# Hybrid decoder block on one core: product order in the up projection, and one head's rounding order

## The chip, the cores and the metric

One of the eight cores of one Trainium2 chip. The metric is the device time of one execution in microseconds (us), the median of the runs. The profiler's recording gives one further execution, with a start and an end for each instruction on TensorE (PE for matmuls, PEld for weight loads), VectorE (DVE), ScalarE (ACT), GpSimd (POOL) and SyncE (SP, which issues DMAs).

## The reference, cut to what matters

One decoder layer over 512 tokens of width 2048, batch 1, all in float32:

```
u    = rmsnorm(x);  proj = u @ w_in               # eight heads of attention, eight of a gated recurrence, two gates
q, k = rmsnorm(q), rmsnorm(k)  per head
y_a  = stick_breaking_attention(q, k, v);  y_b = hgrn2(...)
m    = sigmoid(gate_a) * (y_a @ p_a) + sigmoid(gate_b) * (y_b @ p_b);   h = x + m @ w_o
up   = causal_depthwise_conv(rmsnorm(h) @ w_up)   # 2 x 5632 columns, width 3
out  = h + (silu(gate) * val) @ w_down
```

The change touches two places: the projection of the second head (its q and k norms), and `rmsnorm(h) @ w_up`.

## The kernel before, in words

**Split products.** Every float32 operand of a large matmul is split in two parts that the fast fp32r matmul takes exactly: ACT rounds the raw tile to its high part (`w_hi`, a copy), and DVE subtracts to get the low part (`w_lo`). A product is hi x hi, hi x lo and lo x hi, summed in a PSUM bank.

**Phase 1, heads.** Weights come in units: 128x1024 tiles (512 KB), four places in a ring. PE does 24 matmuls a unit. For each unit ACT calls `split_ahead` (L688, the copy is L686) and DVE its own (L1132, the subtraction is L1129), two units ahead (`LEAD = 2`). A head has 14 units (position `p` in `phase1_body`); a unit's load waits until the unit four before is done on PE. Beside the weights each head has its own small steps, `head_steps`, called behind the rounding of the same position. In the second head (`i == 0`, `hh == 1`) these are on ACT: position 1 squares of q (`squares_of`), 2 the inverse root for q (`inv_sqrt_start`: Ln and Exp, L754 and L756, which wait for DVE's mean, `ms`), 3 three copies for the first head and the squares of k (L760, L762, which wait for DVE's `kn`, L1331), 4 the inverse root for k, 5 the rounding of `S` (L849). On DVE, position 3: `w_lo` of the unit, take k (L1331), squares' low part, then `normed("q")`; position 4: `w_lo`, `select` and the mean of k's squares (L1209); position 5: `w_lo`, `S_lo` (L1349), `normed("k")` (L1213 to L1337). PE's q x k products (L2103) at position 6 wait for the end of `normed("k")`. ACT, DVE and PE work each through its own list in order, and meet at semaphores.

**Phase 4, feed-forward.** A table of 528 slots, each a weight tile in a ring of six. For a pair of output tiles `f` (44 of them) there are eight up slots (`kp` = 0 to 7) and then, in the middle of the run, four down slots. `f` of 7 and more are "wide": 37 of the 44. A wide up slot has seven products (a fast two-by-two scheme, `WIDE_PRODUCTS`), each a bank of its own. `wide_high` (L2268) multiplies a high weight by the high and the low activations in one matmul of 512 columns; `wide_low` (L2274) multiplies the low weight by the high activations, 256 columns into the first half of the bank. Below, "high" and "low" matmuls are these two.

- The order in a slot before: seven highs, a wait for `w_lo` (`w4_ready`), seven lows. In the last slot (`kp == 7`) three highs, three lows, a semaphore `early_done`, four highs, four lows.
- `early_done` lets ACT copy the second halves of banks 0 to 2 (`low_halves`, L1006) and DVE add the first halves (`add_halves`, L1785) while the other four banks are still written; behind the slot's end the same is done for banks 3 to 6 (L1001). Then DVE combines, scales and convolves.
- The down slots (L2359, L2360, L2363, 512 columns each) use banks 7, 0, 1, 7; ACT copies each out (L1037), and the GpSimd queue adds it to `out_t` in HBM.
- SP loads slot `n` once slot `n - 6` is done (L469). DVE at position `n`: for an even slot `n + 3` of a wide `f`, the weight sums of that slot and the next in three operations (L1743, L1746, L1748), which wait for both loads; then `lo_slot(n + 2)` (L1755). So at the position of `kp` = 1 DVE waits for the loads of `kp` = 4 and 5, and only then subtracts `w_lo` for `kp` = 3. ACT rounds `w_hi` three slots ahead (L965).

Of the kernel before, what the change touches and what calls it, by code (L numbers as in the profile page):

```python
# [27 lines left out]
P = 128  # L28
# [19 lines left out]
HEAD_UNITS = 14  # L48
HEAD_TILES = 7
HEADS_PER_BODY = 2  # L50
BODY1 = HEADS_PER_BODY * HEAD_UNITS
# [16 lines left out]
KP = KT // 2  # L68
# [57 lines left out]
EARLY = 3  # L126
# [34 lines left out]
def build_program(nc, x_t, wstream, wgates, wslots, wfirst, params, out_t):  # L161
# [7 lines left out]
    def sb(name, cols, at, dt=F32):  # L169
        return nc.alloc_sbuf_tensor_at(name, [P, cols], dt, offset=base + at)  # L170
# [76 lines left out]
    w4_hi = [sb(f"w4_hi{j}", WC, a + 4 * WC, F32R) for j, a in enumerate(ring_at)]  # L247
# [41 lines left out]
    bank = [banks[:, j * SEQ:(j + 1) * SEQ] for j in range(8)]  # L289
# [50 lines left out]
    w4_step, w4_sums, w4_hi_ready, w4_ready, slot_done = (  # L340
        sem("w4_step"), sem("w4_sums"), sem("w4_hi_ready"), sem("w4_ready"), sem("slot_done"))
    p1_ready, up_out, first_out, a_ready, dve4_step = (
        sem("p1_ready"), sem("up_out"), sem("first_out"), sem("a_ready"), sem("dve4_step"))
    early_done, low_copied, drained = sem("early_done"), sem("low_copied"), sem("drained")
# [93 lines left out]
    def part(t, j, n=1):  # L438
        return t[:, j * HALF:(j + n) * HALF]
# [18 lines left out]
    with nc.Block() as block:  # L458
# [221 lines left out]
        def _(act):  # L680
            steps = Steps(act, act_step)

            def split_hi(n, slot, arrived):
                act.wait_ge(w_in_slot[slot], arrived)
                act.wait_ge(unit_done, n + 1)
                act.activation(w_hi[slot][:, :], w_raw[slot][:, :], ACT.Copy).then_inc(w_hi_ready, 1)  # L686

            def split_ahead(start, i, body, p):  # L688

                q = p + LEAD  # L690
                before = PAIR_SLOTS if start >= START_P else 0
                if isinstance(i, int):
                    n = start + i * body + q
                    if WSLOTS + 1 < n < START4:
                        split_hi(n, n % WSLOTS, 16 * ((n - before) // WSLOTS + 1))
                else:
                    assert start % WSLOTS == 0 and body % WSLOTS == 0
                    split_hi(i * body + (start + q), q % WSLOTS,
                             i * (16 * body // WSLOTS) + 16 * ((start + q - before) // WSLOTS + 1))
# [160 lines left out]
            def phase1_body(i):  # L860
                for hh in range(HEADS_PER_BODY):
                    for p in range(HEAD_UNITS):
                        split_ahead(0, i, BODY1, hh * HEAD_UNITS + p)
                        if not i == hh == 0:
                            head_steps(i, hh - 1, HEAD_UNITS + p)
                        head_steps(i, hh, p)

            for i in range(HEADS // HEADS_PER_BODY):
                phase1_body(i)
# [1118 lines left out]
        def _(pe):  # L1988
# [262 lines left out]
            def bank_free(f, j):  # L2251

                d = GROUP * (f - 3)
                if f == WIDE:
                    if j >= GROUP:
                        pe.wait_ge(down_out, GROUP + d + j - GROUP + 1)
                    return
                pe.wait_ge(drained, 2 * (f - WIDE) - (j < EARLY))
                if j < 2:
                    pe.wait_ge(down_out, GROUP + d + j + 2)  # L2260

            def wide_high(f, kp, ring, j):

                w, x = WIDE_PRODUCTS[j]
                both = v_parts[kp][:, :].rearrange("p (a c) -> p a c", a=2)[:, :, x * HALF:(x + 1) * HALF]
                if kp == 0:
                    bank_free(f, j)
                nc.tensor.matmul(bank[j].rearrange("p (a c) -> p a c", a=2), w4_hi[ring][:, w * P:(w + 1) * P], both,  # L2268
                                 start=kp == 0, stop=False, skip_group_check=True)

            def wide_low(kp, ring, j):

                w, x = WIDE_PRODUCTS[j]
                return nc.tensor.matmul(bank[j][:, 0:HALF], w4_lo[ring][:, w * P:(w + 1) * P], part(v_hi[kp], x),  # L2274
                                        start=False, stop=kp == KP - 1, skip_group_check=True)

            def wide_products(at_, f, kp, ring):

                for j0, j1 in ((0, EARLY), (EARLY, 7)) if kp == KP - 1 else ((0, 7),):
                    for j in range(j0, j1):  # L2280
                        wide_high(f, kp, ring, j)
                    if j0 == 0:
                        pe.wait_ge(w4_ready, at_ + 1)
                    for j in range(j0, j1):
                        ins = wide_low(kp, ring, j)
                    if j1 == EARLY:
                        ins.then_inc(early_done, 1)
                return ins

            def down_free(d):  # L2290
# [15 lines left out]
            def up_slot(n):  # L2306
                _, f, kp = entry(n)
                at_, ring, loads = place(n)
                if f == 0:
                    pe.wait_ge(v_ready, kp + 1)  # L2310
                if f == 1 and kp == 0:
                    pe.wait_ge(rms_ms, 2)
                if f > 1 and kp == 0:
                    pe.wait_ge(up_out, (f - 1))
                if wide(f):
                    pe.wait_ge(w4_hi_ready, at_ + 1)
                    wide_products(at_, f, kp, ring).then_inc(slot_done, 1)
                    return
                pe.wait_ge(w4_ready, at_ + 1)
                for w, x, b, half in PRODUCTS:  # L2320
                    out = bank[4 * (f == 1) + b][:, half * HALF:(half + 1) * HALF]
                    wh, wl = (t[ring][:, w * P:(w + 1) * P] for t in (w4_hi, w4_lo))
                    xh, xl_ = (t[kp][:, x * HALF:(x + 1) * HALF] for t in (v_hi, v_lo))
                    nc.tensor.matmul(out, wh, xh, start=kp == 0 and half == 0, stop=False, skip_group_check=True)  # L2324
                    nc.tensor.matmul(out, wh, xl_, start=False, stop=False, skip_group_check=True)  # L2325
                    ins = nc.tensor.matmul(out, wl, xh, start=False, stop=kp == KP - 1, skip_group_check=True)  # L2326
                ins.then_inc(slot_done, 1)
# [146 lines left out]
```

## Time and profile before

| | |
|---|---|
| median of 3 runs | 2783.75 us (2783.39 to 2783.79) |
| profiled execution: own time, span | 2783.4 us, 2781.9 us |
| granted TensorE clock | 1.000 |
| busy: PE, DVE, ACT | 2775.1, 2109.6, 1285.3 us |
| L2268 high matmuls, 2072 | 531.0 us busy |
| L2274 low matmuls, 2072 | 300.5 us busy |

The span is the time from the first to the last instruction of the recording; what lies around it is 1.5 us. Busy time is the union of an engine's instructions. Matmuls are pipelined and overlap in the rows: a high one lasts 0.39 us in its row while the next starts some 0.23 us behind it. What a matmul takes of the time is therefore read from one start to the next.

### The profile page before, as it was taken

Reading aid. Unit: us, or ns where it says so; the run is one execution under the profiler, and the core shown is the slowest. Engines: PE = TensorE matmul, PEld = TensorE weight load, DVE = VectorE, ACT = ScalarE, POOL = GpSimd, SP = SyncE. Lnnn points to the kernel's source line nnn. Section 1 sums busy time; section 2 is a strip of 40 time slices with the busy share of each in tenths; the row PEclk is TensorE's granted clock in tenths of the full one; section 3 lists DMA queues with packets and bytes.
Section 4 is the critical chain, followed back from the end, with each engine's and each line's share of the span. In section 5 each row is a group of like instructions: output and inputs, shape, how many; then the busy total and the mean of one; then the engine's idle time right before and its main releaser. Section 6 shows DMA issues by size and latency. Waiting matters only on the chain.

```text
span 2781.9 us, 41114 instructions
## 1 busy us (share of the span) xinstructions
PE 2775.1 (100%) x14858; PEld 2403.7 (86%) x14858; DVE 2109.6 (76%) x3543; ACT 1285.3 (46%) x1738; POOL 428.2 (15%) x579
## 2 busy tenths in 40 slices
PE   9999999999999999999999999999999999999999
PEld 7888888888889999888889988888888888888887
DVE  7776777677777878444468988888888888888884
ACT  5444434443433334333345555555555555555554
POOL 2022154324400000000000110111101011110102
PEclk9999999999999999999999999999999999999999
DMA  5464586676534555444455666556556666655657
GB/s 181 144 178 96 176 189 137 176 192 125 112 118 153 168 177 176 143 143 143 137 168 145 149 141 138 139 136 144 135 138 140 138 139 135 144 136 137 140 138 163
DMA packets 187446, 410.97 MB, mean 148 GB/s; under 512 B 22288, under 2 KB 50320, under 8 KB 186128
## 3 DMA queue, kind: packets, MB, share of 16 engines
q1 hardware_dynamic: 120240, 283.90, 33.0%
q0 software_dynamic: 67040, 124.82, 23.8%
q8 instruction: 109, 1.79, 0.3%
q14 instruction: 57, 0.47, 0.0%
HBM read 347.81 MB, written 112.72 MB: 166 GB/s over the span
## 4 chain that ended last, share of the span: by engine, by line
PE 97%; DVE 2%; ACT 1%; issue 0%; DMA 0%; SPq 0%; DVEq 0%; ACTq 0%
PE bank L2268 17%; PE bank L1995 12%; PE bank L1997 12%; PE bank L1996 12%; PE bank L2274 9%; PE bank L2359 6%; PE bank L2360 6%; PE bank L2363 6%; PE bank L2221 3%; PE bank L2222 3%; PE bank L2223 3%; PE bank L2324 2%; PE bank L2326 2%; PE bank L2325 2%; PE bank L2069 1%; PE bank L2103 1%
## 5 line engine op out<-in xcount | busy, mean ns | idle before, releaser
L965 ACT ACTIVATE w_hi<-w_two 128x896 fp32r<-128x896 f32 (+1 forms) x528 | 434.3, 839 | 358.3 <-DVE w_two L1748 311.9
L2268 PE MATMUL bank<-v_parts,w_hi 128*128 128x512 f32 x2072 | 531.0, 392 | 0.0
L1755 DVE TENSOR_TENSOR w_lo<-w_two,w_hi 128x896 fp32r<-128x896 f32 (+1 forms) x528 | 495.9, 952 | 25.4 <-ACT w_hi L965 24.6
L2268 PEld LDWEIGHTS bank<-v_parts,w_hi 128*128 128x128 f32 x2072 | 370.2, 189 | 63.5
L1995 PE MATMUL bank<-u_hi,w_hi 128*128 128x512 f32 x1000 | 395.4, 395 | 0.2 <-DVE w_lo L1129 0.2
L1997 PE MATMUL bank<-u_hi,w_lo 128*128 128x512 f32 x1000 | 389.9, 390 | 0.0
L1996 PE MATMUL bank<-u_lo,w_hi 128*128 128x512 f32 x1000 | 389.3, 389 | 0.0
L1129 DVE TENSOR_TENSOR w_lo<-w_raw,w_hi 128x1024 fp32r<-128x1024 f32 x189 | 230.4, 1222 | 133.4 <-ACT w_hi L686 131.3
L668 POOL DMA_DIRECT2D out_t<-stage x168 | 142.6, 851 | 1161.9 <-ACT stage L1037 1129.5
L2274 PEld LDWEIGHTS bank<-v_parts,w_lo 128*128 128x128 f32 x2072 | 292.4, 190 | 26.3
L2274 PE MATMUL bank<-v_parts,w_lo 128*128 128x256 f32 x2072 | 300.5, 282 | 0.0
L2359 PE MATMUL bank<-s_hi,w_hi 128*128 128x512 f32 x698 | 272.1, 390 | 0.9 <-ACT stage L1037 0.9
L2360 PE MATMUL bank<-s_lo,w_hi 128*128 128x512 f32 x698 | 272.1, 390 | 0.0
L1997 PEld LDWEIGHTS bank<-u_hi,w_lo 128*128 128x128 f32 x1000 | 187.7, 188 | 40.0
L1995 PEld LDWEIGHTS bank<-u_hi,w_hi 128*128 128x128 f32 x1000 | 187.9, 188 | 38.2 <-DVE w_lo L1129 0.8
L1996 PEld LDWEIGHTS bank<-u_lo,w_hi 128*128 128x128 f32 x1000 | 187.9, 188 | 37.7 <-issue 0.2
L686 ACT ACTIVATE w_hi<-w_raw 128x1024 fp32r<-128x1024 f32 x189 | 197.1, 1048 | 16.2 <-DMA w_raw<-wstream 16.1
L2363 PE MATMUL bank<-s_hi,w_lo 128*128 128x512 f32 x698 | 189.1, 389 | 0.0
L1743 DVE TENSOR_TENSOR w_two<-w_two 128x512 f32<-128x512 f32 (+1 forms) x180 | 115.3, 641 | 65.6 <-DMA w_two<-wslots 64.5
L2359 PEld LDWEIGHTS bank<-s_hi,w_hi 128*128 128x128 f32 x698 | 131.2, 188 | 27.2 <-issue 1.3
L2363 PEld LDWEIGHTS bank<-s_hi,w_lo 128*128 128x128 f32 x698 | 131.0, 188 | 27.2
L878 ACT ACTIVATE g_hi<-g_raw 128x896 fp32r<-128x896 f32 x96 | 91.1, 951 | 137.1 <-DVE g_raw L1572 101.4
(303 smaller groups left out, 5266.5 us busy)
## 6 DMA issues: line engine op xcount, KB each, us to landing
w_two<-wslots SPq DMA_DIRECT2D x504, 256.0 KB, 2.7
w_raw<-wstream SPq DMA_DIRECT2D x189, 512.0 KB, 3.5
out_t<-stage POOLq DMA_DIRECT2D x168, 256.0 KB, 4.3
sums_scratch<-wfirst POOLq DMA_DIRECT2D x72, 448.0 KB, 5.6
g_raw<-sums_scratch SPq DMA_DIRECT2D x48, 448.0 KB, 3.3
g_raw<-wgates SPq DMA_DIRECT2D x48, 256.0 KB, 2.9
w_two<-sums_scratch SPq DMA_DIRECT2D x24, 448.0 KB, 3.3
sums_scratch<-sums_scratch POOLq DMA_DIRECT2D x72, 128.0 KB, 4.5
```

The costliest lines, as they stand in the source:

```text
L686: act.activation(w_hi[slot][:, :], w_raw[slot][:, :], ACT.Copy).then_inc(w_hi_ready, 1)
L965: act.activation(w4_hi[ring][:, 0:width], w4_raw[ring][:, 0:width], ACT.Copy).then_inc(w4_hi_ready, 1)
L1129: dve.tensor_tensor(w_lo[slot][:, :], w_raw[slot][:, :], w_hi[slot][:, :].bitcast(F32), ALU.subtract).then_inc(w_ready, 1)
L1755: dve.tensor_tensor(w4_lo[ring][:, 0:width], w4_raw[ring][:, 0:width], w4_hi[ring][:, 0:width].bitcast(F32), ALU.subtract).then_inc(w4_rea ...
L1995: nc.tensor.matmul(out, wh, hi, start=first, stop=False)
L1996: nc.tensor.matmul(out, wh, lo, start=False, stop=False)
L1997: return nc.tensor.matmul(out, wl, hi, start=False, stop=last)
L2268: nc.tensor.matmul(bank[j].rearrange("p (a c) -> p a c", a=2), w4_hi[ring][:, w * P:(w + 1) * P], both, start=kp == 0, stop=False, skip_gr ...
L2274: return nc.tensor.matmul(bank[j][:, 0:HALF], w4_lo[ring][:, w * P:(w + 1) * P], part(v_hi[kp], x), start=False, stop=kp == KP - 1, skip_g ...
L2359: nc.tensor.matmul(out, wh, s_hi[f % 8][:, :], start=first and f == fs[0], stop=False)
L2360: nc.tensor.matmul(out, wh, s_lo[f % 8][:, :], start=False, stop=False)
L2363: ins = nc.tensor.matmul(out, w4_lo[ring][:, k * P:(k + 1) * P], s_hi[f % 8][:, :], start=False, stop=last and f == fs[-1])
```

## The change

Phase 1, ACT: in the second head the roundings for positions 3 and 5 are called at positions 2 and 4, ahead of these positions' `head_steps`. Phase 4, PE: in wide up slots of odd `kp` the seven lows come first, then the seven highs; in the last slot (`kp == 7`) `early_done` is set by the third high. Even slots keep their order. The start and stop flags go along. No instruction is added or removed.

```
--- before.py
+++ after.py
@@ phase1_body, ACT
-                        split_ahead(0, i, BODY1, hh * HEAD_UNITS + p)
+                        early = i == 0 and hh == 1
+                        if not (early and p in (3, 5)):
+                            split_ahead(0, i, BODY1, hh * HEAD_UNITS + p)
+                        if early and p in (2, 4):
+                            split_ahead(0, i, BODY1, hh * HEAD_UNITS + p + 1)
                         if not i == hh == 0:
                             head_steps(i, hh - 1, HEAD_UNITS + p)
                         head_steps(i, hh, p)
@@ wide_high, wide_low: PE
-    nc.tensor.matmul(..., start=kp == 0, stop=False, ...)
+    return nc.tensor.matmul(..., start=kp == 0, stop=kp == KP - 1, ...)
...
-                                        start=False, stop=kp == KP - 1, skip_group_check=True)
+                                        start=False, stop=False, skip_group_check=True)
@@ wide_products: PE
-                for j0, j1 in ((0, EARLY), (EARLY, 7)) if kp == KP - 1 else ((0, 7),):
-                    for j in range(j0, j1):
+                if kp % 2 == 0:
+                    for j in range(7):
                         wide_high(f, kp, ring, j)
-                    if j0 == 0:
-                        pe.wait_ge(w4_ready, at_ + 1)
-                    for j in range(j0, j1):
+                    pe.wait_ge(w4_ready, at_ + 1)
+                    for j in range(7):
                         ins = wide_low(kp, ring, j)
-                    if j1 == EARLY:
-                        ins.then_inc(early_done, 1)
+                else:
+                    pe.wait_ge(w4_ready, at_ + 1)
+                    for j in range(7):
+                        wide_low(kp, ring, j)
+                    for j in range(7):
+                        ins = wide_high(f, kp, ring, j)
+                        if kp == KP - 1 and j == EARLY - 1:
+                            ins.then_inc(early_done, 1)
                 return ins
```

## Rows read from the trace of the kernel before

**Rows 1.** Page, part 1: busy us (share of the span) and instructions of PE.

```profile
PE 2775.1 (100%) x14858; PEld 2403.7 (86%) x14858; DVE 2109.6 (76%) x3543; ACT 1285.3 (46%) x1738; POOL 428.2 (15%) x579
```

**Rows 2.** Waits of PE: us in total, times, longest.

```profile
PE bank L2103 <- DVE kn L1337: 1.1, 1, 1.1
PE bank L2359 <- ACT stage L1037: 0.9, 1, 0.9
```

**Rows 3.** Timeline (start us, us, engine), PE: slots kp 0 to 3 of f = 20.

```profile
2003.34 1.75 PE L2268 MATMUL bank<-v_parts,w_hi 128*128 128x512 f32 x7
2004.92 1.00 PE L2274 MATMUL bank<-v_parts,w_lo 128*128 128x256 f32 x7
2005.75 1.78 PE L2268 MATMUL bank<-v_parts,w_hi 128*128 128x512 f32 x7
...
2010.65 1.78 PE L2268 MATMUL bank<-v_parts,w_hi 128*128 128x512 f32 x7
```

**Rows 4.** Timeline, PE: first and sixth matmul of the down slot behind f = 20.

```profile
2022.88 0.40 PE L2359 MATMUL bank<-s_hi,w_hi 128*128 128x512 f32 x1
...
2024.04 0.39 PE L2360 MATMUL bank<-s_lo,w_hi 128*128 128x512 f32 x1
```

**Rows 5.** Timeline, DVE and PE: second gate slot, which starts at 844.23, all 256 columns.

```profile
842.97 2.09 DVE L1576 TENSOR_TENSOR g_lo<-g_raw,g_hi 128x896 fp32r<-128x896 f32 x2 [4.35 <-ACT g_hi L878]
...
844.23 0.33 PE L2221 MATMUL bank<-u_hi,g_hi 128*128 128x256 f32 x1
844.40 0.28 PE L2222 MATMUL bank<-u_lo,g_hi 128*128 128x256 f32 x1
844.52 0.28 PE L2223 MATMUL bank<-u_hi,g_lo 128*128 128x256 f32 x1
```

**Rows 6.** Timeline, DVE, f = 20: first weight sum for kp 4, 5; low part for kp 3.

```profile
2007.62 0.69 DVE L1743 TENSOR_TENSOR w_two<-w_two 128x512 f32<-128x512 f32 x1 [1.67 <-DMA w_two<-wslots]
...
2009.15 1.08 DVE L1755 TENSOR_TENSOR w_lo<-w_two,w_hi 128x896 fp32r<-128x896 f32 x1
```

**Rows 7.** Timeline, DVE and PE, f = 31: the same two, and the start of slot kp 3.

```profile
2343.61 0.69 DVE L1743 TENSOR_TENSOR w_two<-w_two 128x512 f32<-128x512 f32 x1 [2.63 <-DMA w_two<-wslots]
...
2345.14 1.08 DVE L1755 TENSOR_TENSOR w_lo<-w_two,w_hi 128x896 fp32r<-128x896 f32 x1
...
2345.63 1.78 PE L2268 MATMUL bank<-v_parts,w_hi 128*128 128x512 f32 x7
```

**Rows 8.** Timeline, ACT, last f: the copy out of bank 7 that a down slot waits for.

```profile
2731.85 0.58 ACT L1037 ACTIVATE stage<-bank 128x512 f32<-128x512 f32 x1
```

**Rows 9.** Timeline, ACT, second head: root of q, rounding, squares of k, rounding.

```profile
122.11 0.63 ACT L754 ACTIVATE rs<-ms 128x512 f32<-128x512 f32 x1 [8.54 <-DVE ms L1209]
...
123.31 1.04 ACT L686 ACTIVATE w_hi<-w_raw 128x1024 fp32r<-128x1024 f32 x1
...
126.25 0.63 ACT L760 ACTIVATE sq<-kn 128x512 f32<-128x512 f32 x1 [1.08 <-DVE kn L1331]
...
136.46 1.04 ACT L686 ACTIVATE w_hi<-w_raw 128x1024 fp32r<-128x1024 f32 x1
```

**Rows 10.** Timeline, DVE, second head: two low parts that wait, and k's last step.

```profile
124.39 1.23 DVE L1129 TENSOR_TENSOR w_lo<-w_raw,w_hi 128x1024 fp32r<-128x1024 f32 x1 [2.31 <-ACT w_hi L686]
...
137.54 1.22 DVE L1129 TENSOR_TENSOR w_lo<-w_raw,w_hi 128x1024 fp32r<-128x1024 f32 x1 [2.31 <-ACT w_hi L686]
...
142.39 0.75 DVE L1337 SCALAR_TENSOR_TENSOR kn<-kn,par,tmp 128x512 f32<-128x512 f32 x1
```

**Rows 11.** Timeline, PE, second head: before k's squares, k's squares, q x k.

```profile
127.91 0.39 PE L1997 MATMUL bank<-u_hi,w_lo 128*128 128x512 f32 x1
128.33 0.50 PE L2040 MATMUL bank<-sq_hi,ones_r 128*128 128x512 f32 x1
...
143.20 2.42 PE L2103 MATMUL bank<-qn,kn 128*128 128x512 f32 x8 [1.15 <-DVE kn L1337]
```

**Rows 12.** Page, part 6: issues of one form, KB each, median us from issue to landing.

```profile
w_raw<-wstream SPq DMA_DIRECT2D x189, 512.0 KB, 3.5
```

More of the change, by code:

```diff
@@ L2267, in wide_high @@
                     bank_free(f, j)
-                nc.tensor.matmul(bank[j].rearrange("p (a c) -> p a c", a=2), w4_hi[ring][:, w * P:(w + 1) * P], both,
-                                 start=kp == 0, stop=False, skip_group_check=True)
+                return nc.tensor.matmul(bank[j].rearrange("p (a c) -> p a c", a=2), w4_hi[ring][:, w * P:(w + 1) * P],
+                                        both, start=kp == 0, stop=kp == KP - 1, skip_group_check=True)
             def wide_low(kp, ring, j):
```

## The prediction, made before the changed kernel was run

> **What bounds the kernel now.** I read the page's busy times first, then the waits of PE, then PE's timeline by starts. PE is busy 2775.1 us of a span of 2781.9 [rows 1], so nothing but PE's own list and its few stalls can move the time. The waits of PE hold two of about a microsecond: q x k in the second head waits 1.1 us for k's last step, and a down slot of the last f waits 0.9 us for a copy of ACT [rows 2]. Everything else must come from the spacing of the matmuls. A faster DVE or ACT is worth nothing unless one of these waits ends on it. The sum is made against the profiled execution's own 2783.4 us (the span and 1.5 around it), 0.35 below the median shown; I add 0.35 at the end.
>
> **Part 1, spacing of highs and lows.** From start to start, seven highs that follow 512-column matmuls (kp 0) take 2004.92 - 2003.34 = 1.58 us, and the seven lows behind them 0.83; slots kp 1 and 2, whose highs follow lows, take (2010.65 - 2005.75) / 2 = 2.45, against 2.41 for kp 0 [rows 3]. So a switch from low to high costs about 0.03 us (on finer starts 0.026, spent over the first five highs). The down slots confirm it: their first five matmuls behind the lows take 1.16 us, where five at the pace of the kp 0 highs (0.227) are 1.13 [rows 3, 4]. Lows in a long run go at 0.12 each [rows 5], seven are 0.84, so the seven right behind highs gain 0.01. A pair of switches taken away is therefore worth 0.03 - 0.01 = 0.02.
>
> Before, a wide f had eight such pairs that cost (kp 0 to 7; the extra one inside kp 7 makes that slot no longer than the others). After, highs and lows come in runs of fourteen: four pairs. Four pairs at 0.02 are 0.08 us per f, and 37 wide f give 37 x 0.08 = 3.0 us. Bounds: the 10 ns of the rows allow 0.015 to 0.025 a pair, 2.2 to 3.7 us; and nothing, if kp 0's pace had another reason (a rival below).
>
> By the Trainium skill ("TensorE: Matmul & The Clock Gate", section "Back-to-back issue gap") the isolated gap is N/2.4 + 2.5 ns, which depends on the columns alone: an estimate of 109 and 216 ns in any order, and so nothing gained by this part. The trace has 0.227 and 0.12 and a pace that depends on what went before, so I go by the rows; the rule's consequence stands among the rivals.
>
> **Part 1, the wait that moves forward.** In odd slots `w_lo` is needed at the slot's start, seven highs (1.6 us) earlier. Behind the first low stands all of PE's list. What is ready by then? For kp 0, 2, 4, 6 nothing changes. For kp 1 the low part ends 0.9 to 1.7 us ahead of the slot's start over the 37 f, for kp 7 1.7 us or more. For kp 3 DVE is held up by the loads for kp 4 and 5: it waits 1.67 us for them, sums, and ends `w_lo` for kp 3 at 2009.15 + 1.08 = 2010.23, while the slot starts at 2010.65 [rows 3, 6]: 0.42 us to spare. In f = 31 the load is later (the wait is 2.63) and `w_lo` ends at 2346.22 for a slot that starts at 2345.63: 0.59 too late [rows 7]. The spare time of the 37 kp 3 slots, from pairs of rows like these, has a median of 0.45; six are below 0.2: 0.17, 0.03, -0.12, -0.14, -0.15 and -0.59. The new order brings slot kp 3 0.02 us closer (two switches less on the way). The chain is tied to the end of the slot before kp 0 (which lets the load of kp 5 go), so a stall in one f buys nothing in the next. Slots kp 5 have 0.03 to 0.04 more than kp 3 in every f, and a stall at kp 3 gives them as much again: no second stall.
>
> How early must `w_lo` be there? The nearest row: in the second gate slot, in a run of 256-column matmuls as here, the low part ended near 842.97 + 1.08 = 844.05, 0.18 us ahead of the slot's start at 844.23, and the next matmul came 0.17 behind, where the pace is 0.12 [rows 5]: 0.05 lost. So about 0.22 is needed. The loss is 0.24 minus the spare time: 0.07 + 0.21 + 0.36 + 0.38 + 0.39 + 0.83 = 2.2 us. Bounds: nothing, if the loads land well in that run (their landings vary from run to run), and 5 us with twice as many late ones.
>
> **Part 1, `early_done`.** In kp 7 it used to come after three highs and three lows, 1.05 us into the slot; now after seven lows and three highs, 0.84 + 0.70 = 1.54. ACT's copy of the early banks starts about 0.48 later; behind it are ACT's next rounding and the copy of the late banks, which used to start 0.2 us after the slot's end and will start 0.33 later. DVE's additions move by as much, 0.35. In 36 f DVE's idle wait for the loads (1.67) [rows 6] takes this up, and kp 1 keeps 0.5 us of its 0.9. In the last f the chain runs through to the copy out at 2731.85 [rows 8], for which PE waits 0.9 us [rows 2]: that stall grows by 0.35 us. Bounds 0 to 0.5.
>
> **Part 2, second head.** The wait of 1.15 us ahead of q x k [rows 11] ends with k's last step, 142.39 + 0.75 [rows 10]. Walk it back. DVE's `w_lo` waited 2.31 us twice, at 124.39 and 137.54 [rows 10], both times for a rounding on ACT that stood behind roots (123.31 and 136.46) [rows 9]. ACT had stood idle 8.54 us before the roots of q [rows 9], and the raw tile is there: its load, issued when unit 15 ended (105.3), takes 3.5 us [rows 12]. So the first rounding, 1.04, fits into this idle time near 113.5 and delays no root. Then DVE goes on at 122.1: `w_lo` to 123.3, take k to 123.9; ACT, with its roots and the three copies until 124.2, squares k then instead of at 126.25 [rows 9]. Normed q ends near 129.4 (was 131.5). The second rounding needs unit 21's tile (issued at 120.3, there at 123.8) and goes at 126.4, again in idle time. DVE's position 4 ends at 133.1 (was 135.2), the root of k at 134.4, `S_lo` at 136.5, and normed k at 139.9 instead of 143.1. PE is ready for q x k at 141.9 at the latest, so the stall goes whole, and 2 us of cover remain. No queue is passed: the roundings issue no DMA, and the loads on SP are released by PE.
>
> The price of a stall is more than its wait: behind it the next matmuls are slow as after a switch. k's squares started 0.42 behind the last matmul [rows 11] where the pace is 0.23, 0.19 lost and some 0.13 after it; the first product with `S` lost a little over 0.2 in this way; q x k 1.3 and 0.1 after it. All three inputs come 1.7 us or more earlier. Together 1.9 us gained. Bounds: 1.1 (the wait alone) to 2.1.
>
> **Sum.** 2783.4 - 3.0 + 2.2 + 0.35 - 1.9 = 2781.05, and with 0.35 for the median 2781.4.
>
> **Rivals.**
> - *Late low weights in nearly every f* (not faster). If PE, which takes instructions in ahead of their turn, has to have `w_lo` some 0.6 us ahead, the typical spare 0.42 [rows 3, 6] falls short by 0.2 in 37 f (7 us), and the late six bring 2 more than counted. It decides from a need of 0.35 on. For it: DVE is within half a microsecond in most f. Against it: the gate slot lost 0.05 at 0.18 to spare [rows 5]. Time: 2783.75 - 3.0 - 1.9 + 0.35 + 2.2 + 6 to 7 = about 2788.
> - *The order is worth nothing*: kp 0's highs are quick for another reason than what precedes them, and the fourteen-runs go at the old pace. The down slots' slow first five [rows 4] speak against it. Time: 2781.4 + 3.0 = 2784.4. This is also what the skill's gap rule ("Back-to-back issue gap") would give.
> - *No late loads*: DMA landings in that run leave kp 3 in time everywhere. Time: 2781.4 - 2.2 = 2779.2. The typical f has time to spare [rows 6], but six outliers in 37 are not likely to vanish together.
> - *Part 2 does nothing*, because k's chain is then held by another step. Its cover of 2 us speaks against it. Time: 2783.3.
>
> **Chances.** Forecast 0.58, late nearly everywhere 0.12, order worth nothing 0.08, no late loads 0.18, part 2 idle 0.04. Range 2779.0 to 2785.0: it holds the forecast with both bounds of most terms, the second, third and fourth rival, and leaves out the first and part of the extremes. A change below 0.2% (5.6 us, 2778.2 to 2789.3) can't be told from none with this measurement; all cases lie inside, so 0.92 for the same; faster needs gains beyond every bound, 0.05; slower a first rival with a need of 0.8 us, 0.03.
>
> **What would show it.** In PE's timeline: highs of even slots starting as 1.58 us for seven, fourteen lows near 1.67, a wide f 0.08 us shorter where nothing stalls; waits of PE on `w_lo` L1755 (shifted by the new lines), few and all at kp 3; no wait for `kn`; the wait of the last f near 1.3. Wrong would be: waits on `w_lo` in most f, stalls at kp 1, or an even slot's highs still taking 1.61.

## The result and the profile after

| | before | after |
|---|---|---|
| median of 22 runs each | 2783.6 us (2783.02 to 2784.05) | 2787.5 us (2785.0 to 2788.99) |
| profiled execution: own time, span | 2783.4, 2781.9 us | 2788.83, 2787.3 us |

The ratio is 1.0014, 95% interval 1.0008 to 1.002. The change costs 3.9 us (0.14%), and the interval doesn't reach 1. The result is outside the forecast range (2779.0 to 2785.0), and close to what the first rival gave (2788). The granted clock is 1.000 in both.

The page of after, its span and the busy times of the engines, answers to [rows 1]:

```profile
span 2787.3 us, 41262 instructions
PE 2778.0 (100%) x14858; PEld 2405.9 (86%) x14858; DVE 2103.7 (75%) x3543; ACT 1278.5 (46%) x1738; POOL 428.0 (15%) x579
```

The waits of PE in after (total us, times, longest us) answer to [rows 2]:

```profile
PE bank L2278 <- DVE w_lo L1759: 2.5, 4, 1.1
PE bank L2368 <- ACT stage L1041: 1.3, 1, 1.3
```

The wait for `kn` is gone and the last f's is 1.3, both as forecast. New are four waits for `w_lo`, 2.5 us. These four can't explain a run that is about 8.5 us above the forecast without stalls (worked out below). The rest shows only in the starts. PE's timeline of f = 20 in after (start, us, line, count) answers to [rows 3]; the last row is cut by the window:

```profile
2003.58 1.75 PE L2272 MATMUL bank<-v_parts,w_hi 128*128 128x512 f32 x7
2005.16 1.84 PE L2278 MATMUL bank<-v_parts,w_lo 128*128 128x256 f32 x14
2006.84 3.36 PE L2272 MATMUL bank<-v_parts,w_hi 128*128 128x512 f32 x14
2010.04 2.12 PE L2278 MATMUL bank<-v_parts,w_lo 128*128 128x256 f32 x14
2011.99 2.23 PE L2272 MATMUL bank<-v_parts,w_hi 128*128 128x512 f32 x9
```

The lows of `kp` 0 and 1 take 2006.84 - 2005.16 = 1.68 us, as forecast. The lows of `kp` 2 and 3, same count and same columns, take 2011.99 - 2010.04 = 1.95. The 0.27 us between them is a stall at the first low of `kp` 3. The view of waits doesn't list it, since a matmul's row overlaps its successor's start by about 0.17 us and no clear idle time is left. On starts, 36 of the 37 wide f stall there: the eight up slots of an f take 19.77 us in the mean, where the one f that doesn't stall (f = 41) takes 19.49 and an f of before 19.55.

The chain that makes `w_lo` late, f = 20 of before (ACT, DVE and GpSimd; in square brackets the idle time before and what ended it). With [rows 6] it is complete:

```profile
1992.08 0.96 DVE L1785 TENSOR_TENSOR early_sum<-bank,early_sum 128x768 f32<-128x768 f32 x1 [1.82 <-ACT early_sum L1006]
2000.29 0.69 DVE L1851 TENSOR_TENSOR a_gate<-a_gate,r_tok 128x512 f32<-128x512 f32 x1
2001.01 0.82 ACT L1019 ACTIVATE y_gate<-a_gate,par 128x512 f32<-128x512 f32 x1 [1.14 <-DVE a_gate L1851]
2001.73 0.58 ACT L1037 ACTIVATE stage<-bank 128x512 f32<-128x512 f32 x1
2002.60 0.85 POOL L668 DMA_DIRECT2D out_t<-stage  x1 [2.43 <-ACT stage L1037]
```

and the same chain in after, whose last two rows answer to [rows 6]:

```profile
1992.83 0.96 DVE L1789 TENSOR_TENSOR early_sum<-bank,early_sum 128x768 f32<-128x768 f32 x1 [2.62 <-ACT early_sum L1010]
2000.89 0.69 DVE L1855 TENSOR_TENSOR a_gate<-a_gate,r_tok 128x512 f32<-128x512 f32 x1
2001.61 0.82 ACT L1023 ACTIVATE y_gate<-a_gate,par 128x512 f32<-128x512 f32 x1 [1.13 <-DVE a_gate L1855]
2002.33 0.58 ACT L1041 ACTIVATE stage<-bank 128x512 f32<-128x512 f32 x1
2003.21 0.85 POOL L668 DMA_DIRECT2D out_t<-stage  x1 [2.43 <-ACT stage L1041]
2008.32 0.69 DVE L1747 TENSOR_TENSOR w_two<-w_two 128x512 f32<-128x512 f32 x1 [1.85 <-DMA w_two<-wslots]
2009.85 1.08 DVE L1759 TENSOR_TENSOR w_lo<-w_two,w_hi 128x896 fp32r<-128x896 f32 x1
```

Against the start of the f's first up slot (2003.34 before, 2003.58 after) the early addition goes from -11.26 to -10.75, DVE's scaling (`a_gate`) from -3.05 to -2.69, ACT's third copy out of the down slots from -1.61 to -1.25, and its store to `out_t` from -0.74 to -0.37. The loads that DVE waits for are issued as before (+0.34 for the second), yet they land later: the weight sums start at +4.74 where they started at +4.28. `w_lo` for `kp` 3 ends at 2010.93; the slot would have started at 2010.04 + 7 x 0.12 = 2010.88.

So the new `early_done` reaches the loads: through DVE's scaling, ACT's convolution term, the copy that stands behind this term in ACT's list, and a store that now overlaps a load more. That is theory A. Theory B says that the order of the products itself makes `w_lo` late, by an earlier need or by what PE does to the loads, and `early_done` is a bystander.

The second head in after. DVE answers to [rows 10], PE to [rows 11].

```profile
132.61 1.22 DVE L1133 TENSOR_TENSOR w_lo<-w_raw,w_hi 128x1024 fp32r<-128x1024 f32 x1
138.71 0.75 DVE L1341 SCALAR_TENSOR_TENSOR kn<-kn,par,tmp 128x512 f32<-128x512 f32 x1
```
```profile
127.53 0.39 PE L2001 MATMUL bank<-u_hi,w_lo 128*128 128x512 f32 x1
127.75 0.39 PE L2044 MATMUL bank<-sq_hi,ones_r 128*128 128x512 f32 x1
140.94 2.32 PE L2107 MATMUL bank<-qn,kn 128*128 128x512 f32 x8
```

ACT in the second head of after answers to [rows 9]; each row holds two roundings, the position's own and the one moved ahead:

```profile
112.15 2.00 ACT L686 ACTIVATE w_hi<-w_raw 128x1024 fp32r<-128x1024 f32 x2
124.92 1.99 ACT L686 ACTIVATE w_hi<-w_raw 128x1024 fp32r<-128x1024 f32 x2
```

Normed k ends at 139.46 instead of 143.14, and DVE's two waits of 2.31 are gone. k's squares follow 0.22 behind the last matmul, where it was 0.42, and q x k starts 143.20 - 140.94 = 2.3 us earlier, with no stall. Not all of this is the change: the start of an execution varies by a microsecond (the 51st matmul of PE starts at 13.00 us in before, at 12.63 in after, and between 12.35 and 13.67 over all traces here), and these 0.4 us are still there at the 501st. From the 501st to the 701st matmul, with the second head's stalls between them, before takes 159.14 - 112.71 = 46.43 us and after 156.79 - 112.31 = 44.48: the head is worth 1.95 us.

### The profile page after: what moved, and what is told of

It reads as the page before. It is cut to its first block, busy times and chain, and to the rows that moved or that the text cites. A ratio compares the mean times of both kernels' runs of the same rounds, so it can differ in the third digit from the quotient of the medians.

```text
span 2787.3 us, 41262 instructions
## 1 busy us (share of the span) xinstructions
PE 2778.0 (100%) x14858; PEld 2405.9 (86%) x14858; DVE 2103.7 (75%) x3543; ACT 1278.5 (46%) x1738; POOL 428.0 (15%) x579
## 4 chain that ended last, share of the span: by engine, by line
PE 96%; DVE 2%; DMA 1%; ACT 1%; issue 0%; SPq 0%; DVEq 0%
PE bank L2272 16%; PE bank L1999 12%; PE bank L2001 12%; PE bank L2000 12%; PE bank L2278 9%; PE bank L2368 6%; PE bank L2369 6%; PE bank L2372 6%; PE bank L2225 3%; PE bank L2227 3%; PE bank L2226 3%; PE bank L2333 2%; PE bank L2335 2%; PE bank L2334 2%; PE bank L2073 1%; DMA w_two<-wslots 1%
## 5 line engine op out<-in xcount | busy, mean ns | idle before, releaser
L2272 PE MATMUL bank<-v_parts,w_hi 128*128 128x512 f32 x2072 | 503.7, 391 | 0.0
L2272 PEld LDWEIGHTS bank<-v_parts,w_hi 128*128 128x128 f32 x2072 | 379.5, 188 | 72.7
L2278 PEld LDWEIGHTS bank<-v_parts,w_lo 128*128 128x128 f32 x2072 | 269.8, 191 | 19.9 <-ACT w_hi L969 7.0
L2278 PE MATMUL bank<-v_parts,w_lo 128*128 128x256 f32 x2072 | 278.6, 284 | 3.2 <-DVE w_lo L1759 2.5
L2369 PEld LDWEIGHTS bank<-s_lo,w_hi 128*128 128x128 f32 x698 | 131.0, 188 | 27.0
```

What stands on the lines that cost most here:

```text
L2272: return nc.tensor.matmul(bank[j].rearrange("p (a c) -> p a c", a=2), w4_hi[ring][:, w * P:(w + 1) * P], both, start=kp == 0, stop=kp == K ...
L2369: nc.tensor.matmul(out, wh, s_lo[f % 8][:, :], start=False, stop=False)
```

## The experiments

Each kernel was timed beside the kernel before, on the same chip. Diffs are against the kernel after, unless said otherwise. Event times below are medians over the 37 wide f, against the start of the first up slot; "sums" is the start of the weight sums for `kp` 4 and 5, which is 0.09 us after the later of their two loads has landed, wherever DVE waits for it.

**The parts apart.** First the second head alone (phase 4 as before):

```
             def wide_products(at_, f, kp, ring):
-                if kp % 2 == 0: ...                    # the new order
+                for j0, j1 in ((0, EARLY), (EARLY, 7)) if kp == KP - 1 else ((0, 7),):
...
```

> The kernel before with the second head's two roundings moved ahead, the up projection as before. Two theories on the change's 10 us of lost time in the wide slots. Theory A (store meets load): early_done comes 0.5 us later, so DVE's additions and scaling end 0.36 later, so ACT's copy out behind the gate's conv term, and the store it lets go, are 0.36 later and run beside the load for kp 5, which lands 0.4 later and makes the low part for kp 3 late in nearly every f. Theory B (order itself): the lows in front need their weights earlier, or slots of the new order let loads and DVE go later, wherever early_done stands. Both theories leave the head out, so both expect here: no wait for kn, PE 2.3 us ahead by the end of the heads (from the trace of the changed kernel: 1083.56 against 1081.2 at the projections behind the gates), no change later. 2783.6 - 2.3 = 2781.3 us.

Measured: 2781.65 us (2781.03 to 2781.99) beside 2783.57, ratio 0.9993 (0.9984 to 1.0002). The profile has no wait for `kn` and 0.9 in the last f; from the 501st to the 701st matmul it takes 44.44 us. The interval reaches 1, but all eleven runs lie below all those of before beside them (2783.05 to 2784.23). Part 2 is worth the 1.9 us of the forecast, so part 1 must have cost what is missing. Then the order alone (roundings of the second head as before):

```
-                        early = i == 0 and hh == 1
...
+                        split_ahead(0, i, BODY1, hh * HEAD_UNITS + p)
```

> The kernel before with the up projection's new order, the second head as before. Both theories: the wide slots as in the changed kernel, 36 of 37 f stall at kp 3 for 0.27 us in the mean (10 us), 3.0 us gained by fewer switches, 0.35 lost in the last f, and the head's 1.1 us wait for kn is back. 2787.5 + 2.3 = 2789.8 us.

Measured: 2787.72 us (2786.42 to 2790.42), ratio 1.0015 (1.0006 to 1.0024); q x k waits 1.2 us for `kn` again. That is 4.15 above before, 2 us less than expected. The expectation put the head at 2.3 instead of 1.95. The stalls of its profiled execution were smaller (the up slots of the 37 wide f take 729.5 us, in after 731.4). Loads land differently from run to run; the interval on each of these ratios is 2.5 us wide to either side, so whether the parts really fail to add up stays open.

**`early_done` late, order untouched.** Before, with the semaphore set two highs later in the last slot, which is nearly when the change sets it:

```
# against the kernel before
                     for j in range(j0, j1):
-                        wide_high(f, kp, ring, j)
+                        ins = wide_high(f, kp, ring, j)
+                        if j0 == EARLY and j == EARLY + 1:
+                            ins.then_inc(early_done, 1)
...
-                    if j1 == EARLY:
-                        ins.then_inc(early_done, 1)
```

> The kernel before with one difference: in the last up slot early_done is set two high matmuls later (behind the fifth high, about 0.46 us later), the order of products unchanged. Theory A: DVE's additions 0.3 to 0.36 us later, the third store of an f as much later, the loads for kp 5 land 0.4 later, the low part for kp 3 ends about 0.45 us later against the slot's start (0.47 to spare falls to about 0); since the highs still come first in kp 3, PE does not stall, but for the last f's wait (0.9 to about 1.3): 2783.6 + 0.3 = 2783.9 us. Theory B: load landings and the low part for kp 3 as before, 0.47 to spare.

```profile
2002.04 0.58 ACT L1037 ACTIVATE stage<-bank 128x512 f32<-128x512 f32 x1
2002.91 0.85 POOL L668 DMA_DIRECT2D out_t<-stage  x1 [2.42 <-ACT stage L1037]
2007.73 0.69 DVE L1743 TENSOR_TENSOR w_two<-w_two 128x512 f32<-128x512 f32 x1 [1.55 <-DMA w_two<-wslots]
2003.33 1.75 PE L2268 MATMUL bank<-v_parts,w_hi 128*128 128x512 f32 x7
```

Measured: 2783.96 us (2783.3 to 2784.78), ratio 1.0002 (0.9993 to 1.0011). The old order needs `w_lo` only behind the highs, so the time can't move; the events can, and do. In f = 20 above the copy starts at -1.29 and the store at -0.42; over all f the sums go from 4.24 to 4.60, and `w_lo` would stand a median 0.10 us ahead of slot `kp` 3, where it stood 0.47. With the products in the old order, the late semaphore alone brings the loads in 0.37 us later. Theory A holds here; B has no place for this.

**The copy ahead of the convolution term.** If the delay passes through the copy's place behind ACT's term, then moving the term behind the copy must cut it:

```
-                    if q == KP + 2:
-                        conv_term(n, f, 0)
...
+                        conv_term(n, f, 0)             # one position later, behind the third copy
```

> The changed kernel with one difference on ACT: for f of 6 to 42 the gate's conv term moves from position kp + 2 behind the slots to position kp + 3, behind that position's copy out, so that the third copy out of an f no longer waits for DVE's scaling. Theory A: the third copy starts about 1.3 us earlier (near -2.5 us from the start of kp 0 instead of -1.25), its store is mostly through when the load for kp 5 is issued, the load lands in 2.7 to 3.3 us instead of 4.3, the low part for kp 3 is in time, no or few waits of PE on w_lo: 2783.6 - 2.3 - 3.0 + 0.35 = 2778.7 us. Theory B: the stalls stay, 2787.5 us.

```profile
2000.14 0.60 ACT L1041 ACTIVATE stage<-bank 128x512 f32<-128x512 f32 x1 [0.58 <-PE bank L2371]
2001.03 0.85 POOL L668 DMA_DIRECT2D out_t<-stage  x1 [1.18 <-ACT stage L1041]
2002.66 1.75 PE L2271 MATMUL bank<-v_parts,w_hi 128*128 128x512 f32 x7
2006.86 0.69 DVE L1746 TENSOR_TENSOR w_two<-w_two 128x512 f32<-128x512 f32 x1 [1.22 <-DMA w_two<-wslots]
```

Measured: 2781.17 us (2779.83 to 2783.02), ratio 0.9991 (0.9982 to 1.0). The copy now waits for PE and no longer for DVE, the store goes at -1.63 and the sums start at 3.96. The median stall is gone, but in the profiled execution four f (9, 12, 28, 31) still lose 3.9 us together. That execution took 2783.02, the slowest of the eleven; without these stalls it would be at 2779.1, near the expected 2778.7 (which put the head at 2.3 instead of 1.95), so such stalls are the likely reason for the miss. One edit on ACT, far from PE, recovers 6.3 us of the change: theory B can't say why.

**Less in the last slot.** `kp` 7 as three lows, three highs, `early_done`, four lows, four highs, so that the semaphore comes as early as before:

```
-                    for j in range(7):
-                        wide_low(kp, ring, j)
-                    for j in range(7):
-                        ins = wide_high(f, kp, ring, j)
+                    for j0, j1 in ((0, EARLY), (EARLY, 7)) if kp == KP - 1 else ((0, 7),):
+                        for j in range(j0, j1):
+                            wide_low(kp, ring, j)
+                        for j in range(j0, j1):
+                            ins = wide_high(f, kp, ring, j)
...
```

> The changed kernel with the last up slot in the order three lows, three highs, early_done, four lows, four highs, so that early_done comes 1.06 us into the slot as in the kernel before (instead of 1.54). Theory A: DVE's additions, the third store (issued 0.735 us ahead of kp 0) and the landing of the load for kp 5 (weight sums at about 4.25) go back to the times of before, and the loss at kp 3 falls from 0.27 us per f to that of the late outliers, 2 to 4 us in all; the last f's wait is 0.9 again: 2783.6 - 1.9 (head) - 2.7 (switches) + 2 to 4 = 2781 to 2783 us. Theory B (the order itself makes the weights late): stalls as in the changed kernel, 2787.5 us.

```profile
2000.13 0.85 POOL L668 DMA_DIRECT2D out_t<-stage  x1 [2.42 <-ACT stage L1041]
2000.85 1.75 PE L2272 MATMUL bank<-v_parts,w_hi 128*128 128x512 f32 x7
2004.95 0.69 DVE L1747 TENSOR_TENSOR w_two<-w_two 128x512 f32<-128x512 f32 x1 [1.48 <-DMA w_two<-wslots]
2007.31 1.84 PE L2278 MATMUL bank<-v_parts,w_lo 128*128 128x256 f32 x14
2008.98 3.36 PE L2272 MATMUL bank<-v_parts,w_hi 128*128 128x512 f32 x14
```

Measured: 2780.7 us (2779.56 to 2782.6), ratio 0.999 (0.9981 to 0.9999). Store at -0.72, sums at 4.20, the lows of `kp` 2 and 3 in 1.67 again, the last f's wait back at 0.9. Six f stall (19, 29, 31, 32, 33, 37; about 2.5 us), and the prediction counted six and 2.2 us for loads that land as in before. This is the order of the change with `early_done` where it was, and it does what the forecast said.

**The order of DVE.** In after the subtraction for `kp` 3 stands behind the sums, which wait for the loads. Put ahead of them, the loads don't matter to it:

```
+                if wide(f) and q == 1:
+                    lo_slot(n + 2)
+                    sums(n + 3)
+                else:
...
```

> The changed kernel with one difference on DVE: at the position of kp 1 in wide f the low part for kp 3 comes ahead of the weight sums of kp 4 and 5, so it no longer waits for the load for kp 5. Theory A: that load still lands late (sums near 4.7 us), but the low part for kp 3 ends near 4.0 us behind the start of kp 0, over 3 us before the slot, kp 5 gains a microsecond, and PE has no wait on w_lo but for a rare one: 2783.6 - 1.9 - 3.0 + 0.35 = 2779.0 us. Theory B: PE's stalls at kp 3 stay, at or above 2785 us.

```profile
2000.17 0.85 POOL L668 DMA_DIRECT2D out_t<-stage  x1 [2.43 <-ACT stage L1041]
2000.55 1.75 PE L2276 MATMUL bank<-v_parts,w_hi 128*128 128x512 f32 x7
2003.36 1.08 DVE L1759 TENSOR_TENSOR w_lo<-w_two,w_hi 128x896 fp32r<-128x896 f32 x1
2005.26 0.69 DVE L1747 TENSOR_TENSOR w_two<-w_two 128x512 f32<-128x512 f32 x1 [0.82 <-DMA w_two<-wslots]
```

Measured: 2780.48 us (2779.07 to 2780.87), ratio 0.9988 (0.9979 to 0.9997). The loads are as late as in after (sums at 4.68), but `w_lo` is 3.4 us ahead of its slot. Of the stalls only two are left, at `kp` 5 (0.45 and 0.22 us). The median stands 1.5 us above the expected 2779.0, the profiled execution (2779.69) 0.7; why the other executions are slower isn't known.

**Both mends together** (the last two edits):

> Both mends on the changed kernel: the mixed last slot and the low part for kp 3 ahead of the sums. Theory A: no wait on w_lo, the last f's wait 0.9, a little less gained from switches (2.7): 2783.6 - 1.9 - 2.7 = 2779.0 us, as far as can be told the same as with the second mend alone. Theory B: above 2785 us.

Measured: 2780.0 us (2778.8 to 2780.91), ratio 0.9987 (0.9978 to 0.9996), 3.5 us ahead of before beside it and 7.5 ahead of after. One f stalls (0.7 us), and the last f waits 0.9. Expected was 2779.0, one microsecond less. It is the fastest of the kernels that compute everything, though the step from the one before it is within the error.

**`kp` 3 back in the old order.** If the late `w_lo` is what PE waits for, this should mend `kp` 3; the question was what `kp` 5 does:

```
-                if kp % 2 == 0:
+                if kp % 2 == 0 or kp == 3:
```

> The changed kernel with slot kp 3 alone back in the old order (highs first). Theory A: the low part for kp 3 is then needed 1.6 us later and is in time; the low part for kp 5 has only 0.04 us more to spare than the one for kp 3, so the stalls move to the start of kp 5 and are a little smaller (some 0.2 us per f), 0.02 to 0.04 us per f of switches come back: 2787 us, within 1. Theory B': kp 3 is a case of its own (its bank or its place in the ring), and the stalls go: 2779.5 us.

Measured: 2786.28 us (2784.76 to 2787.44), ratio 1.0009 (1.0 to 1.0018). No stall at `kp` 3, but now slots `kp` 4 and 5 take 2.58 and 2.51 us in the mean (before: 2.45 each): the low part for `kp` 5, DVE's next, is as late for its slot as that for `kp` 3 was. DVE's whole sequence is late, and the first slot that begins with lows pays.

**The store cut short.** This run tests the last link, from the store to the load: the third store of a wide f moves 32 of its 512 columns, so 480 columns of those tiles are missing in the output. All else, `early_done` included, is as in after.

```
-                pool.dma_start(out_t[:, c * SEQ:(c + 1) * SEQ], buf[:, :], accum_op=ALU.add).then_inc(done, 16)
+                w = 32 if wide(d // GROUP + 2) and d < END and d % GROUP == 2 else SEQ
+                pool.dma_start(out_t[:, c * SEQ:c * SEQ + w], buf[:, 0:w], accum_op=ALU.add).then_inc(done, 16)
```

> The changed kernel with the third accumulating store of each wide f cut from 512 to 32 columns a partition (the other 480 columns of these tiles are left out of the output); its place in the GpSimd queue, its issue time (-0.37 us from the start of kp 0) and all waits stay. Theory A (this store's transfer delays the load for kp 5): the load issued at +0.34 lands at its median of 2.7 to 3.0 us, the weight sums start near 3.5 us instead of 4.7, PE has no waits on w_lo but rare ones, 2779 to 2780 us. Rival (the load is late for another reason: the load for kp 4 in front of it, or the second store): sums stay at 4.4 to 4.7 and so do the stalls, 2786 to 2788 us.

```profile
2000.43 0.85 POOL L669 DMA_DIRECT2D out_t<-stage  x1 [2.42 <-ACT stage L1042]
2000.80 1.75 PE L2273 MATMUL bank<-v_parts,w_hi 128*128 128x512 f32 x7
2004.00 0.69 DVE L1748 TENSOR_TENSOR w_two<-w_two 128x512 f32<-128x512 f32 x1 [0.29 <-DMA w_two<-wslots]
2005.53 1.08 DVE L1760 TENSOR_TENSOR w_lo<-w_two,w_hi 128x896 fp32r<-128x896 f32 x1
```

Measured: 2779.13 us (2778.79 to 2779.84), ratio 0.9984 (0.9975 to 0.9993). The store is issued at the same -0.37, the sums start at 3.21, 1.5 us earlier than in after (the load lands at 3.10 instead of 4.59), and `w_lo` is never less than 0.46 us ahead of `kp` 3. No f stalls, the six outliers of before are gone too, and the spread of the runs falls from 4.0 us (22 runs) to 1.05 (11 runs).

The records of DMA packets show how the store gets in the way. From 1.0 to 2.5 us behind the start of f = 20, by queue: packets, MB, share of the time of the 16 DMA engines. The GpSimd queue with the store is `q0`, SP's with the loads `q1`. First after:

```profile
q0 software_dynamic: 62, 0.13, 97.1%
q1 hardware_dynamic: 10, 0.02, 3.8%
```

then with the store cut short:

```profile
q1 hardware_dynamic: 132, 0.25, 61.0%
q0 software_dynamic: 144, 0.02, 41.2%
```

The store's packets hold all 16 DMA engines (178 ns a packet of 2 KB in the median, one in ten 0.5 us or more), and the load's hardly get a turn. Once they do, they are as quick as ever: 84 ns in both kernels. Over the 37 f the store's last packet ends at a median of 3.86 us and the load lands at 4.59; in before 3.20 and 4.14. The two go together f by f (correlation 0.96 in after, 0.97 in before). The six late loads that the prediction found in before are of the same kind: their stores are issued when the others are, but end at 3.77 to 4.65, all others by 3.50.

## Why the prediction was wrong

**Spacing: right.** An f without a stall takes 19.493 us for its up slots and 10.880 for its down slots, before 19.546 and 10.908: 0.080 us saved per f, 3.0 us in all. That the order of highs and lows has a price is thereby shown. The formula of the Trainium skill ("TensorE: Matmul & The Clock Gate", section "Back-to-back issue gap"), which the page gives for the isolated gap and which depends on the columns alone, doesn't describe this stream of matmuls with a weight load each: 227 and 120 ns here, and five slower ones behind each switch. The rival "order is worth nothing" falls, and the time of the run with the cut store confirms the sum: before, less 1.9 and 3.0, plus 0.35, is 2779.05; it took 2779.13. The size of the whole change, 3.9 us, is below the 0.2% within which the prediction put every case, though with 22 runs each it can be told from no change.

**How early `w_lo` is needed: right.** Behind a stall the slot starts 0.15 us after `w_lo` ends, and 0.06 more is lost in the slot: 0.21, forecast 0.22. The first rival was priced by a need of 0.6 us and is wrong in its mechanism; that its 2788 lies next to the measured 2787.5 is chance. `w_lo` wasn't needed earlier than forecast, it came later.

**`kp` 1 keeps 0.5 us: right**, 0.53 at the least over the 37 f. **`kp` 5 has little more to spare than `kp` 3: right**, as the run with `kp` 3 in the old order shows. **Second head: right**, 1.9 us timed with this part alone, 1.95 in the traces from the 501st to the 701st matmul. **Last f: right**, 0.9 to 1.3.

**The step that failed** is the sentence on `early_done`: "In 36 f DVE's idle wait for the loads (1.67) [rows 6] takes this up". The 0.35 us of delay on DVE were right (0.36 measured), and DVE does idle there. But the delay doesn't end on DVE. ACT's convolution term waits for DVE, the third copy out stands behind the term, and the accumulating store behind the copy is issued 0.37 us later, which moves it into the time of the load that DVE's idle wait is for. The wait was counted as a cushion; instead its end moved, by 0.45 us. Between the median spare time (0.45) and what must be kept (0.22) there were only 0.23 us: 36 f stall where six were counted.

In numbers: the term "late `w_lo`" was +2.2 us, with bounds 0 and 5. In the timed runs it is 2787.5 - 2779.05 = 8.5; in the profiled execution 37 x (19.766 - 19.493) = 10.1. The run with `early_done` kept early measures what the forecast described: 2780.7, against 2781.4 forecast.

What is shown and what isn't: the path from `early_done` to the store (moved by two edits at different places, each with the time that follows), and from the store to the landing (its size cut, the load early). The packets show that the load waits for the DMA engines that the store holds. Why a packet of the store holds its engine for 0.18 to 0.5 us, and why a few stores take a microsecond longer than the rest, no run tells.

## What to carry to other kernels

Idle time of an engine is a cushion only if the thing that ends it stands still: when a step moves later, follow it through every engine to the DMAs that it releases, and ask whether one of them shares its time with the load that the idle engine waits for. If a margin is under half a microsecond, look whether an operation that doesn't need the load stands in a list behind one that does; swapping the two bought more margin (3.4 us ahead of the slot) than even the cut store did (1.5). And where matmul rows overlap, read a stall from the starts of equal groups, not from the list of waits: 36 of them, some 10 us in all, appeared there as four with 2.5.

## What the runs showed of the hardware

- An accumulating store of 256 KB holds up a load that runs beside it, and over these kernels more the later it is issued. The load was issued at +0.34 us in every kernel:

| kernel | third store issued | its last packet ends | sums start |
|---|---|---|---|
| copy ahead of the term | -1.63 us | 2.66 us | 3.96 us |
| before | -0.73 | 3.20 | 4.24 |
| last slot mixed | -0.72 | 3.15 | 4.20 |
| before, `early_done` late | -0.42 | 3.59 | 4.60 |
| after | -0.37 | 3.86 | 4.68 |
| after, store cut to 32 columns | -0.37 | 2.14 | 3.21 |

  From -1.63 to -0.37, the store's 1.26 us of delay bring 0.72 us on the load; without its bulk the load is 1.5 us earlier.
- After a switch from 256-column to 512-column matmuls the starts are 233, 236, 228, 232 and 231 ns apart before the 227 of the steady pace: 25 ns per switch, spread over five matmuls. In the other direction nothing is lost (seven lows are 7 x 120 ns or a little less).
- Where PE waits for late loads, the kernel's time is unsteady: the 22 runs of before span 1.0 us, the 22 of after 4.0, and the 11 with the store cut short 1.05.
